# Eight modulation tiles per layer moved from the feed-forward up stage into attention, and column-half down stages

## What is computed

```python
# block one, each layer
h = h + mixer(rms_norm(h, attn_norm[l]))
h = h + (silu(conv(n @ w_up gate)) * (n @ w_up up)) @ w_down[l]
# block two, each layer: six vectors of 1024 for the latent, six for the context
mod_l = split(silu(c) @ ada_w[l] + ada_b[l], 6)
mod_c = split(silu(c_ctx) @ ada_w[l] + ada_b[l], 6)
h = rms_norm(x, g) * (1 + scale) + shift          # shift, scale, gate from mod
x = x + gate * (mix(h) @ w_out);  x = x + gate2 * (conv_ffn(h2) @ ffn_down)
```

## Time and profile before

| | us |
|---|---|
| median of three runs | 2127.74 |
| lowest, highest | 2122.54, 2133.12 |
| profiled execution, its own time | 2131.4 |
| its span in the profile | 2129.6 |
| mix 1.0, to the norm's transposes | 35.1 to 217.5 |
| up and down 1.0 | 217.5 to 380.0 to 455.9 |
| mix 1.1 | 455.9 to 641.6 |
| up and down 1.1 | 641.6 to 804.0 to 885.3 |
| block two | 885.3 to the end |

### The profile page before, as it was taken

One profiled execution on the slowest core, in us unless ns is written; L12 is line 12 of the kernel. 1 busy time (PEld: TensorE's weight loads), 2 busy tenths in 40 slices (PEclk: granted clock), 3 DMA queues, 4 the chain that ended last, 5 costly groups with the idle time before them and its releaser, 6 DMA issues.

```text
span 2129.6 us, 26140 instructions
## 1 busy us (share of the span) xinstructions
PE 1915.3 (90%) x10107; PEld 1522.5 (71%) x10107; DVE 790.7 (37%) x1668; ACT 874.6 (41%) x1548; POOL 940.4 (44%) x412
## 2 busy tenths in 40 slices
PE   3999899999779999798879979999998778989997
PEld 2666788777558887697544667888887655669986
DVE  2433332134323321437265444433211663444431
ACT  3543444345444444442334534444321323445652
POOL 2732566766224767343202033444443331035876
PEclk9998899999878999899885989999999887998999
DMA  4422798543127985232100022333222331024653
GB/s 159 159 80 64 239 304 284 217 145 132 60 74 242 303 280 209 84 102 72 60 0 1 1 79 80 99 94 92 92 97 82 91 90 57 1 79 122 187 166 138
DMA packets 248988, 261.91 MB, mean 123 GB/s; under 512 B 13330, under 2 KB 199794, under 8 KB 242594
## 3 DMA queue, kind: packets, MB, share of 16 engines
q1 hardware_dynamic: 247746, 255.62, 37.8%
q10 hardware_dynamic: 1120, 4.63, 0.5%
HBM read 259.18 MB, written 1.05 MB: 122 GB/s over the span
## 4 chain that ended last, share of the span: by engine, by line
PE 79%; DVE 10%; ACT 3%; DMA 3%; issue 2%; SPq 1%; POOL 0%; DVEq 0%; ACTq 0%
PE bank L340 21%; PE bank L341 20%; PE bank L342 19%; PE bank L649 4%; PE bank L672 3%; PE bank L1217 2%; PE bank L657 2%; PE bank L395 1%; PE bank L909 1%; PE bank L935 1%; ACT weights_high L327 1%; PE bank L1561 1%; DVE big L592 1%; DMA weights<-in_ffn_w_down 1%; DVE x_tokens L515 1%
## 5 line engine op out<-in xcount | busy, mean ns | idle before, releaser
L334 POOL TENSOR_TENSOR weights_low<-weights,weights_high 128x1024 fp32r<-128x1024 f32 (+2 forms) x392 | 921.9, 2367 | 1081.8 <-ACT weights_high L327 1081.5
L327 ACT ACTIVATE weights_high<-weights 128x1024 fp32r<-128x1024 f32 (+2 forms) x392 | 400.7, 1036 | 521.7 <-PE bank L342 152.0
L340 PE MATMUL bank<-normed_features_high,weights_high 128*128 128x256 f32 (+1 forms) x1408 | 449.8, 319 | 6.3 <-DVE normed_features_low L424 6.0
L341 PE MATMUL bank<-normed_features_high,weights_low 128*128 128x256 f32 (+1 forms) x1408 | 441.2, 313 | 0.0
L342 PE MATMUL bank<-normed_features_low,weights_high 128*128 128x256 f32 (+1 forms) x1408 | 440.8, 313 | 0.0
L340 PEld LDWEIGHTS bank<-normed_features_high,weights_high 128*128 128x128 f32 x1408 | 272.8, 194 | 65.4 <-issue 36.2
L340 PE MATMUL bank<-weights_high,normed_features_high 128*128 128x512 f32 (+4 forms) x688 | 285.1, 414 | 30.5 <-POOL weights_low L334 17.3
L342 PEld LDWEIGHTS bank<-normed_features_low,weights_high 128*128 128x128 f32 x1408 | 273.5, 194 | 14.1
L341 PEld LDWEIGHTS bank<-normed_features_high,weights_low 128*128 128x128 f32 x1408 | 273.8, 194 | 13.6
L341 PE MATMUL bank<-weights_high,normed_features_low 128*128 128x512 f32 (+4 forms) x688 | 271.9, 395 | 0.0
L342 PE MATMUL bank<-weights_low,normed_features_high 128*128 128x512 f32 (+4 forms) x688 | 270.6, 393 | 0.0
(11 more groups left out here) (240 smaller groups left out, 2246.7 us busy)
## 6 DMA issues: line engine op xcount, KB each, us to landing
work<-in_ada_w SPq DMA_DIRECT2D x48, 1024.0 KB, 7.9
weights<-in_ffn_w_up SPq DMA_DIRECT2D x44, 1024.0 KB, 6.2
weights<-in_ffn_up SPq DMA_DIRECT2D x44, 1024.0 KB, 5.9
weights<-in_ffn_w_down SPq DMA_DIRECT2D x22, 1024.0 KB, 4.9
weights<-in_ffn_down SPq DMA_DIRECT2D x21, 1024.0 KB, 5.0
weights<-in_diff_w_qkv SPq DMA_DIRECT2D x12, 1024.0 KB, 5.0
weights<-in_hyb_w_in SPq DMA_DIRECT2D x10, 1024.0 KB, 5.2
weights<-in_even_w_in SPq DMA_DIRECT2D x8, 1024.0 KB, 5.0
```

The costliest lines, as they stand in the source:

```text
L327: A.eng.activation(high(whigh[:, m % HIGHS, :]), raw(wslot[:, u % SLOTS, :]), ACT.Copy).then_inc(scalar_done, A.one(("A", "high", m)))
L334: G.eng.tensor_tensor(raw(wlow[:, u % SLOTS, :]), raw(wslot[:, u % SLOTS, :]), high(whigh[:, m % HIGHS, :]).bitcast(F32), ALU.subtract).th ...
L340: T.eng.matmul(out_, lh, rh, start=first, stop=False)
L341: T.eng.matmul(out_, ll, rh, start=False, stop=False)
```

## The change

Eight of the 24 tiles of each layer (group 0) are consumed in the mix, at eight new places between the attention turns of the second half of the heads (`MIDDLE`: A is a tile, O an output unit). The other 16 stay in the up stage, one behind each of the pieces 2 to 17. The SP queue's list changes with it. Tile buffers, banks and a scratch row move so that they are free there. The down stages of 256 tokens go by column halves. The last two splits into the next phase are left to that phase.

```diff
+        def add_ada(first, count):
+            issue.extend(("ada", first + n) for n in range(count))
...
                     stream.append((w[r * 512:r * 512 + 512, c * 512:c * 512 + 512].rearrange("(k p) n -> p k n", p=P),
                                    lambda s: s.rearrange("p (k n) -> p k n", k=4)))
+                    if first_ada is not None and (r, c) == (1, 1):
+                        add_ada(first_ada + 2, ADA_EARLY - 2)
                     issue.append(("weights", len(stream) - 1))
+                    if first_ada is not None and (r, c) == (0, 0):
+                        add_ada(first_ada, 2)
...
-        ADA_AFTER = [2 if f >= FC - 2 else 1 for f in range(FC)]
-        ADA_N = KT * 3
-        ada_slot = [work[:, 0:SLOT], work[:, SLOT:2 * SLOT]]
+        ADA_N, ADA_EARLY = KT * 3, KT
+        ADA_AFTER = [1 if 2 <= f < 2 + ADA_N - ADA_EARLY else 0 for f in range(FC)]
+        ada_slot = [work[:, 2048:2048 + SLOT], qkt[:, 4096:4096 + SLOT]]
...
                 issue.append(("weights", len(stream) - 1))
-                if ada is not None and f >= 2:
-
-                    issue.extend(("ada", first + n) for n in ([0, 1] if f == 2 else [f - 1] if f < FC - 1 else range(f - 1, ADA_N)))
...
+                if ada is not None and f < ADA_N - ADA_EARLY:
+                    add_ada(first + ADA_EARLY + f, 1)
...
-        add_down_rows("1.0 ffn down", io["ffn_w_down"][0])
+        add_down_halves("1.0 ffn down", io["ffn_w_down"][0])
...
-        add_down_rows("1.1 ffn down", io["ffn_w_down"][1])
+        add_down_halves("1.1 ffn down", io["ffn_w_down"][1])
...
-        add_down_rows("2.1 ffn down", io["ffn_down_2"][1])
+        add_down_halves("2.1 ffn down", io["ffn_down_2"][1])
...
+        MIDDLE = "AAAAOAOAAAOO"
+
+        def out_order(ada):
+
+            units = [(r, c, q) for r in range(2) for c in range(2) for q in range(2)]
+            both = [u + (j,) for u in units for j in range(2)]
+            if not ada:
+                return both
+            first, order, tile = iter(both), [], 0
+            for what in MIDDLE:
+                order.append(next(first) if what == "O" else None)
+            return order + list(first)
+
+        def out_T(T, ph, tiles, banks, free, left, ready, layer):
+
+            wh = wl = m = None
+            tile = 0
+            for unit in out_order(layer is not None):
+                if unit is None:
+                    if tile == 0:
+                        e, step = free(ADA_BANK[0])
+                        T.eng.wait_ge(SEM[e], done(*step))
+                    ada_tile_T(T, WITH_ADA[layer], tile, layer)
+                    tile += 1
+                    yield
+                    continue
...
+                if r == 0 and q == 0:
+                    e, step = free(banks[n])
+                    T.eng.wait_ge(SEM[e], done(*step))
+                    if layer is not None and banks[n] == ADA_BANK[0]:
+                        T.eng.wait_ge(vector_done, done("V", WITH_ADA[layer], "rows", 0))
...
+        def out_V(V, ph, tiles, banks, layer):
+            for unit in out_order(layer is not None):
...
+                if unit is not None and unit[0] == 0 and layer is not None and unit in ((0, 0, 1, 0), (0, 0, 1, 1)):
+                    part = 2 * unit[3]
+                    ada_rows_V(V, WITH_ADA[layer], layer, (0,), (part, part + 1))
+                yield
...
         def up_T(T, ph, lo, n, ada, normed):
-            tile = 0
+            tile = ADA_EARLY
...
-                if f in (KT + 1, 2 * KT + 1):
-                    ada_rows_V(V, ph, WITH_ADA.index(ph), (f // KT - 1,))
+                if f == KT + 3:
+                    ada_rows_V(V, ph, WITH_ADA.index(ph), (1,))
...
+            k = len(tiles)
+            for half in range(2):
+                for f0 in range(0, FC, 2):
...
                     wh, wl, m = take_half(T)
...
+                    for c in range(2):
+                        f = f0 + c
...
+                        for j in range(k):
+                            i = product(T, psum[banks[k * half + j]][:, :], (hidh(f, n)[:, tok(j)], hidl(f, n)[:, tok(j)]), (wh[:, c, :], wl[:, c, :]),
                                         f == 0, f == FC - 1)
...
-                ahead(A, first_half[ph] + steps * (c + 1) + HIGHS)
+                ahead(A, first_half[ph] + steps * (c + 1) + HIGHS - (2 if c + 1 == count // steps else 0))
...
+        ADA_BANK = (1, 5, 6)
...
-            squares=work[:, 2048 + 512 * (2 * half + t):2560 + 512 * (2 * half + t)] if last else None,
+            squares=gate[:, 1024 + 512 * t:1536 + 512 * t] if last else None,
...
+            OUT_BANKS = (2, 3, 0, 1)
...
-              [(24, 0), (8, 8), (16, 34), (8, 12), (8, 32), (8, 0)],
+              [(24, 0), (8, 8), (16, 34), (8, 12), (16, 32), (8, 0)], 0,
...
-              [(16, 0), (8, 8), (24, 44), (0, 8), (4, 24), (4, 14), (8, 6)],
+              [(16, 0), (8, 8), (24, 44), (16, 46), (8, 6)], 1,
...
                 if what == "ada":
-                    if u % ADA_N < 2:
-
-                        sp.wait_ge(tensor_done, done("T", ("1.0 norm2", "1.1 norm2")[u // ADA_N], "k", KT - 1))
+                    if u < 2:
+
+                        sp.wait_ge(vector_done, done("V", "end", "setup"))
                     else:
                         sp.wait_ge(tensor_done, done("T", "ada", u - 2))
                     sp.dma_start(ada_slot[u % 2], ada_stream[u]).then_inc(ada_full[u % 2], 16)
```

More of the change, by code:

```diff
@@ new lines, in out_order @@
+        def out_order(ada):
[19 more added lines that the diff above has]
+                    continue
+                r, c, q, j = unit
+                t, n = tiles[j], len(tiles) * c + j
+                if j == 0:
+                    wh, wl, m = take_half(T)
+                if r == 0 and q == 0:
[3 more added lines that the diff above has]
+                        T.eng.wait_ge(vector_done, done("V", WITH_ADA[layer], "rows", 0))
+                for kk in range(2):
+                    k = 4 * r + 2 * q + kk
+                    if c == 0 and j == 0:
+                        T.eng.wait_ge(vector_done, done(*ready(k)))
+                    i = product(T, psum[banks[n]][:, :], left(k, t), (wh[:, kk, :], wl[:, kk, :]), k == 0, k == KT - 1)
+                if j == len(tiles) - 1:
+                    half_read(T, i, m)
+                    if r == 1 and q == 1:
+                        T.note(("T", ph, "piece", n))
+                elif r == 1 and q == 1:
+                    i.then_inc(tensor_done, T.one(("T", ph, "piece", n)))
+                yield
@@ new lines, in out_A @@
+        def out_A(A, ph, tiles, banks, layer):
+            for unit in out_order(layer is not None):
+                if unit is None:
+                    yield
+                    continue
+                r, c, q, j = unit
+                t, n = tiles[j], len(tiles) * c + j
+                if r == 1 and q == 1:
+                    if n == 0:
+                        A.eng.activation(stat[:, 32:33], const("ident", 0, 1), ACT.Sqrt).then_inc(scalar_done, A.one())
+                    A.eng.wait_ge(vector_done, done("V", ph, "x", n))
+                    A.eng.activation(psum[banks[n]][:, :], xt[:, t, c * 512:c * 512 + 512], ACT.Square, scale=D ** -0.5,
+                                     accum_out=stat[:, 2 * t + c:2 * t + c + 1]).then_inc(scalar_done, A.one(("A", ph, "squares", n)))
+                if j == len(tiles) - 1:
+                    ahead(A, first_half[ph] + 4 * r + 2 * c + q + 1 + HIGHS)
+                yield
@@ L1194, in ahead_and_squares @@
+                T.note(("T", ph, "out", half))
         def ahead_and_squares(A, ph, parts, steps, count):
@@ L1221, in ada_tile_T, with ada_rows_V @@
                 T.note(("T", ph, "rows", g))
-        def ada_rows_V(V, ph, layer, groups):
+        def ada_rows_V(V, ph, layer, groups, parts=range(4)):
             V.eng.wait_ge(adab_in, 16 * 8 * 2)
@@ L1227, in ada_rows_V @@
                 V.eng.wait_ge(tensor_done, done("T", ph, "rows", g))
-                for j in range(4):
+                for j in parts:
                     r = slice(32 * j, 32 * j + 2 + 2 * layer)
@@ L1906, in mix_T @@
                 norm_T(T, nm, tiles)
-                weave(both(in_T(T, ph_in, cuts, pieces, IN_BANKS, nm, between), out_T(T, ph_out, tiles, IN_BANKS, freed, left, out_needs)),
+                weave(both(in_T(T, ph_in, cuts, pieces, IN_BANKS, nm, between), out_T(T, ph_out, tiles, OUT_BANKS, freed, left, out_needs, layer)),
                       steps_T(T, ph, jobs), plan)
@@ L1918, in mix_A @@
                 norm_evac_A(A, nm, tiles)
[L1919 removed]
+                weave(both(in_read(A, ph_in, cuts, pieces, IN_BANKS, dst, direct, after_A), out_A(A, ph_out, tiles, OUT_BANKS, layer)),
                       steps_A(A, ph, jobs, aside_A), plan)
```

74 lines of the change are left out of this document (26 added, 48 removed).

## The result

| | us |
|---|---|
| before, median of 4 runs | 2126.64 (2122.54 to 2133.12) |
| after, median of 4 runs | 2494.03 (2486.92 to 2503.54) |
| ratio | 1.1727 (95%: 1.1675 to 1.178) |
| profiled run after, its span | 2490.32, 2488.5 |
| predicted | 2514 (2435 to 2600) |

What follows compares the result with a forecast made beforehand. TensorE, busy 90% of the span, was taken to bound the kernel. 28 x (12.4 + 2.15) = +407 and -21.5 for other parts gave +386 on 2131.4 us, 2517, less 3.7 to the median: 2514 us (2435 to 2600).

Steps and rivals of the forecast that it cites:

- The wait and its place: Up stages: SP waits for a tile consumed behind piece f, holding the weights of f+1; 14 per layer, 28 in all.
- Rival 1: SP queue in the up stages is not held, only the small parts stay: 2106 us; chance 5%.
- 12.4 us for a hold: Up stages: TensorE idle per hold, from SP waking 0.1, tile and weights landing 8.6, splits and gaps 3.63.
- The 2.5 us for a tile ahead: Up stages: a tile issued ahead of a piece's weights adds 2.5 us to their 6.1 us landing.
- rival 4: Up stages: the tile ahead does not delay the weights, 70 us less, 2444 us; chance 7%.
- The clock term, 2.15 for each: Up stages: TensorE restarts at half clock after each hold, losing 2.15 us each, 60 in all.
- Rival 2: TensorE's clock stays low in the held pieces, 133 us more, 2647 us; chance 8%.
- rival 3: Clock costs little after holds: 2454 us, or 2475 at most by the Trainium skill's rule; chance 10%.
- The other parts, -21.5: Everything besides the holds, across up stages, mix, down stages, kernel's end and held splits: -21.5 us together.
- Column halves: Down stages of 256 tokens: +3 us for short ring slots, -3 us for fewer adds at the kernel's end.
- held splits: Two splits left to the next phase: -6 us at residual adds, later splits cost more; sum -2 us.
- The tiles in the mix, +10: Mix: tiles cost +6 us in layer 0, +2 in layer 1, VectorE's adds +1 per layer; +10 us.

Runs made afterwards that it cites:

- e1_order: Changed kernel with each up-stage tile queued three pieces later, behind a later piece's weights, all other edits kept: 2102.53 us, 0.9881 of before.
- g2_before_held: Kernel before with only the SP queue's order changed, each tile asked for three pieces earlier, so that 36 weights are held: 2607.68 us, 1.2258 of before.
- e3_weights_first: Changed kernel with SP waiting at the same place, but then issuing the next piece's weights ahead of the tile: 2434.05 us, 1.144 of before.
- e2_lead_one: Changed kernel, queue order as changed, with the up stage's tiles consumed one piece earlier: 2208.4 us, 1.0379 of before.
- e2b_lead_two: Changed kernel, queue order as changed, with the up stage's tiles consumed two pieces earlier: 2095.9 us, 0.9859 of before.
- e4_busy: Changed kernel with 84 unused TensorE products added behind the tile of each piece from 2 to 15: 2504.5 us, 1.1771 of before.
- e4b_busier: Changed kernel with 100 unused TensorE products added behind the tile of each piece from 2 to 15: 2452.65 us, 1.1524 of before.
- g1_output_first: e1_order with one output unit put ahead of the first tile in layer 0's mix: 2098.48 us, 0.9888 of before.

## Why the prediction was right, and where it was off

- **The wait and its place**: right. Weights of pieces 3 to 16 are held, 28 in all, in the two up stages only; e1_order and g2_before_held show that the order in the queue is the cause by itself. Rival 1 falls. The signs came as written: waits of up to 19.7 us in the queue (15 to 20 said), up stages of 344 and 346 us (some 350 said), and no idle time before the down stages.
- **12.4 us for a hold**: measured 12.16, so 340 us instead of 347. Its parts came out one by one. Counted as in the prediction, from the tile's issue, the weights took 8.5 us to land (416.42 to 424.92) in place of 8.6, and the splits 3.64 in place of 3.63; SP woke at once. The rest is rounding, since 0.1 + 8.6 + 3.63 is 12.33. The 2.5 us for a tile ahead came from two tiles and a down transfer; e3_weights_first prices it at 2.1 to 2.35, and rival 4 falls.
- **The clock term, 2.15 for each**: the term that was mis-sized. Measured 1.25 to 1.5, so 35 to 41 us instead of 60. I took half of the mean of two stretches at half clock, 2.97 and 5.60 us. In the 28 pieces the stretch lasted 2.9 to 5.1 us, mean 3.35, and it cost a little under half of that. Rival 2 (clock stays low) and rival 3 (it costs little) both fall: the clock came back in every piece, and it cost about 40 us, twice the 21 that rival 3 allowed at most.
- **The other parts, -21.5**: e1_order has -24.3. Tiles out of the up stages and the idle time before the down stages went as said. Column halves came out at some -5 where I had 0, held splits at -4 where I had -2, neither resolved by the medians; at the end of the kernel two residual adds are left where there were four, and three adds of block two's output stages that took 2.2 to 2.6 us beside a split take 0.69 now, the one of the earlier trace rows with 2.19 among them. Against that, the wait in 1.1's projection was 3.07 us where I had +2.7, and that in 2.0's 1.1.
- **The tiles in the mix, +10**: the mix of layer 0 grew by 7.6 us and that of layer 1 by -0.8, which together is 3 us under the sum; its reason was incomplete. My working for these tiles looked at their loads and at the output weights behind them and left out the bank: the first tile waits 3.3 us for ScalarE's read of bank 1, and of the 11.7 us that the eight tiles take in layer 0 (four of 1.88, four of 1.04) only some 4 are seen in the stage's length, where I had +6 and +1.
- **The sum as a whole**: 340 + 41 - 24 is 357, the profiled executions differ by 359, and the medians by 367. So the forecast of +386 is 27 to 29 us too high by its own terms (19 of them the clock, 7 the idle time, 3 the other parts), and only 19 to 20 by the medians: the rest of its closeness is luck, for no term of the sum stands for those 8 to 10 us. The four executions of the changed kernel spread over 16.6 us and those of before over 10.6, and the two profiled ones differ in stages that the change hardly touches: the mix of 2.0 is 14.1 us longer than before, and that of 2.1 some 10 shorter. The same stretch of the mix of 2.0, first of the change, then of before:

```profile
1445.00:1545.00 100.00, 89.53 (x285) 49.57 (x285) 56.02 (x178) 33.41 (x110) 18.35 (x16) 0.60 0.00 1
```

```profile
1085.00:1185.00 100.00, 91.50 (x327) 49.49 (x326) 57.47 (x181) 39.96 (x128) 18.35 (x16) 0.68 0.00 1
```

  TensorE gets through 285 matmuls instead of 327, at a granted clock of 0.60 instead of 0.68. That is no effect of an edit in this stage: eight kernels run the same program in it (the change, e1_order, e2_lead_one, e2b_lead_two, e3_weights_first, e4_busy, e4b_busier and g1_output_first), and it takes 376.8 to 395.3 us in their traces. The length goes with the stage's granted clock: 0.85 to 0.87 in e2b_lead_two (376.8), e4b_busier (378.1) and g1_output_first (380.5), 0.82 to 0.84 in the five others (385.0 to 395.3); before has 0.86 and 379.1. Why the clock differs there from one execution to another stays open; no run was made for it.

## What to carry to other kernels

A queue that issues in order turns every wait in it into a wait of all that stands behind. When a load is moved or added, write down for each entry which finished step it waits for, and when the entry behind it is due; if the first comes later than one full latency ahead of the second, the latency lands on the engine that does the work, once for each turn. Here 28 such places cost 391 us, with all transfers unchanged in number and size, and a shift of the tiles by two pieces undid it; half of that lead already took away three quarters of the cost, since two pieces' loads under way together shared one latency. And before a stage's length is put down to an edit, compare it over kernels that have the same program there: the mix of 2.0 differed by up to 18 us between such runs.

## What I had not expected of the hardware

- Idle times of only some 2 to 3 us, once in 21 us, in a stretch where TensorE was busy for 177 of 200 us (e4_busy), were followed by the half clock in 22 of 28 turns; pieces took 7.2 us there, against 7.4 behind 12 us of idle time. The length of the idle time alone did not decide it: one of 1.84 us was followed by half clock, and one of 3.58 us was not.
- The clock's share in what 28 interruptions cost is small beside the idle time itself, 35 to 41 of some 380 us. The return to full speed took no fixed time: behind idle times that were all 12.0 to 12.4 us it came after 5.1 and 4.7 us in the first held piece of the two up stages and after 2.9 to 3.1 in the last of them, and in e2_lead_one once after 5.7.
